# Two-layer hybrid encoder trunk: weights ahead of the second token tile, GpSimd's loads behind ten split chunks, and four splits placed elsewhere in the engines' orders

## What is computed

```python
for i in range(2):
    x = LN(alpha*x + 0.5 * swiglu(x, ffn_w_in[i,0], ffn_w_out[i,0]))        # 1024 -> 2816 -> 1024
    x = LN(alpha*x + token_mix(x, w_in[i], ..., w_br[i], w_out[i]))         # four gated mixers
    x = LN(alpha*x + 0.5 * swiglu(x, ffn_w_in[i,1], ffn_w_out[i,1]))
    x = LN(alpha*x + sigmoid(x @ ple_gate_w[i] + b) * (p[i] @ ple_w[i]))    # embedding
```

## Time and profile before

| what | us |
|---|---|
| three runs | 1456.32, 1460.9, 1455.49; median 1456.32 |
| the profiled execution | 1455.92 |
| its span, first to last instruction | 1454.1 |
| TensorE busy (matmul) | 1420.6 (98%) |
| VectorE busy | 975.9 (67%) |
| ScalarE busy | 664.2 (46%) |
| mean granted TensorE clock | 0.994 |

### The profile page before, as it was taken

How to read it: one execution, slowest core, us unless ns; L and a number is a source line. 1 busy time by engine, 2 the same in 40 slices (tenths; PEclk the granted TensorE clock), 3 DMA queues, 4 the chain that set the end, 5 groups by cost and what they waited for, 6 DMA issues and landing times.

```text
span 1454.1 us, 23318 instructions
## 1 busy us (share of the span) xinstructions
PE 1420.6 (98%) x10174; PEld 1324.2 (91%) x10174; DVE 975.9 (67%) x1085; ACT 664.2 (46%) x653; POOL 53.6 (4%) x100
## 2 busy tenths in 40 slices
PE   8999999999999999999989999999999999999996
PEld 6999989999998889999779999899999998999985
DVE  4544577899786865445874545768997858545477
ACT  4444335664545444443444344347535354443441
POOL 5000000000000010000000000000000001000000
PEclk9999999999999999999999999999999999999999
DMA  9756545546544576565465665554456455755641
GB/s 313 226 183 194 174 150 170 176 151 219 168 129 157 191 245 198 184 193 174 155 221 183 194 189 188 174 175 145 169 179 175 132 174 181 229 184 193 198 150 58
DMA packets 168054, 263.34 MB, mean 181 GB/s; under 512 B 8958, under 2 KB 101456, under 8 KB 167952
## 3 DMA queue, kind: packets, MB, share of 16 engines
q1 hardware_dynamic: 163616, 249.66, 53.3%
q0 software_dynamic: 4336, 12.20, 2.6%
HBM read 260.77 MB, written 1.05 MB: 180 GB/s over the span
## 4 chain that ended last, share of the span: by engine, by line
PE 88%; DVE 7%; DMA 2%; ACT 1%; SPq 0%; issue 0%; DVEq 0%; ACTq 0%
PE ps L1250 27%; PE ps L1252 27%; PE ps L1251 27%; PE ps L1452 3%; DVE wlo L773 3%; DMA raw<-in_ffn_w_in 2%; DVE big L901 2%; PE ps L1276 1%; PE ps L1278 1%; ACT whi L544 1%; PE ps L1281 1%; PE ps L1317 1%; DVE big L837 0%; DVE xlo L814 0%; DVE xtok L842 0%
## 5 line engine op out<-in xcount | busy, mean ns | idle before, releaser
L773 DVE TENSOR_TENSOR wlo<-raw,whi 128x2048 fp32r<-128x2048 f32 x230 | 525.0, 2289 | 334.2 <-ACT whi L544 333.9
L1250 PE MATMUL ps<-xhi,whi 128*128 128x256 f32 x2336 | 658.8, 282 | 3.3 <-DVE S L788 3.3
L544 ACT CAST whi<-raw 128x2048 fp32r<-128x2048 f32 x230 | 438.3, 1909 | 487.1 <-PE ps L1252 455.1
L1252 PE MATMUL ps<-xhi,wlo 128*128 128x256 f32 x2336 | 655.7, 281 | 0.0
L1251 PE MATMUL ps<-xlo,whi 128*128 128x256 f32 x2336 | 655.6, 281 | 0.0
L1250 PEld LDWEIGHTS ps<-xhi,whi 128*128 128x128 f32 x2336 | 441.2, 189 | 6.7 <-DVE wlo L773 2.2
L1251 PEld LDWEIGHTS ps<-xlo,whi 128*128 128x128 f32 x2336 | 441.0, 189 | 1.5
L1252 PEld LDWEIGHTS ps<-xhi,wlo 128*128 128x128 f32 x2336 | 440.9, 189 | 0.0
L1250 PE MATMUL ps<-whi,bh 128*128 128x512 f32 x368 | 146.8, 399 | 2.0 <-DVE blo L804 2.0
L1252 PE MATMUL ps<-whi,blo 128*128 128x512 f32 x368 | 145.2, 395 | 0.0
L1251 PE MATMUL ps<-wlo,bh 128*128 128x512 f32 x368 | 144.7, 393 | 0.0
(11 more groups left out here) (241 smaller groups left out, 1209.0 us busy)
## 6 DMA issues: line engine op xcount, KB each, us to landing
raw<-in_ffn_w_in SPq DMA_DIRECT2D x172, 512.0 KB, 5.0
raw<-in_w_in SPq DMA_DIRECT2D x140, 512.0 KB, 4.5
raw<-in_ffn_w_out SPq DMA_DIRECT2D x88, 512.0 KB, 4.4
raw<-in_w_br SPq DMA_DIRECT2D x32, 512.0 KB, 5.2
raw<-in_w_out SPq DMA_DIRECT2D x16, 512.0 KB, 4.2
raw<-in_ple_gate_w SPq DMA_DIRECT2D x16, 512.0 KB, 4.5
gv<-in_ln_g POOLq DMA_DIRECT2D x8, 512.0 KB, 4.9
b_bc<-in_ln_b POOLq DMA_DIRECT2D x8, 512.0 KB, 6.1
```

The lines of the kernel that those rows point to most:

```text
L544: nc.scalar.copy(whi[:, slot, :], raw[:, source, :]).then_inc(whi_made, 1)
L773: nc.vector.tensor_tensor(wlo[:, slot, :], raw[:, source, :], whi[:, slot, :].bitcast(F32), ALU.subtract).then_inc(wlo_made, 1)
L1250: nc.tensor.matmul(dst, a_hi, b_hi, start=start, stop=False, skip_group_check=True)
L1252: return nc.tensor.matmul(dst, a_lo, b_hi, start=False, stop=stop, skip_group_check=True)
```

## The change

It has five parts. (1) SyncE loads token tile 1 between chunk 0 and chunk 1, not ahead of chunk 0; TensorE turns tile 1 behind the first pass of tile 0, and ScalarE and VectorE split it behind all four half chunks. TensorE runs 14 instead of 8 products of ones behind its first turn. (2) GpSimd waits for ten split chunks ahead of its 37 DMAs. (3) In step 5 of the mixers the subtraction of the mean stands ahead of both `los` calls. (4) At step 0 of a feed-forward half the sixth chunk is split behind the hidden part, on both engines. (5) In norm i=2 the third gate chunk is subtracted ahead of x's tile 1; in the last norm the next layer's chunk 1 is cast ahead of quarter 2's sigmoid and subtracted between quarter 2's gate and its product, and `low_x` of tile 0 stands behind quarter 3's gate.

```diff
@@ SyncE
+                        if c0 + gu_at(j) + kk == 0:
+                            sp.dma_start(xtok[:, 1, :], x[0, P:T, :]).then_inc(x_in[1], 16)
-            for t in range(TT):
-                sp.dma_start(xtok[:, t, :], x[0, P * t:P * t + P, :]).then_inc(x_in[t], 16)
+            sp.dma_start(xtok[:, 0, :], x[0, 0:P, :]).then_inc(x_in[0], 16)
@@ GpSimd
             link(nc.gpsimd.memset(wbd[:, :, :], 0.0))
+            pool.wait_ge(wlo_made, 10)
@@ ScalarE, ffn at j == 0
-                        his(g + RING + 2)
                         if middle is not None:
                             middle()
                         act.wait_ge(h0_T, n0 // NFF + 1)
                         nc.scalar.copy(hhi[0], ...).then_inc(hhi_made, 1)
+                        his(g + RING + 2)
@@ ScalarE, start (VectorE alike, with low_x and head_low)
             split_x(0, 0)
-            head(0)
-            head(1)
+            for i in range(4):
+                head(i)
             split_x(0, 1)
-            head(2)
-            head(3)
@@ ScalarE, last norm
                     if a == 2:
-                        his(base + CHUNKS + 1)
-                    if a == 3:
                         his(base + CHUNKS + 2)
-                        if l + 1 < DEPTH:
-                            split_x(4 * l + 4, 0)
+                    if a == 3 and l + 1 < DEPTH:
+                        split_x(4 * l + 4, 0)
@@ VectorE, ffn
-                    if j == 0:
-                        los(g + RING + 2)
-                        if middle is not None:
-                            middle()
+                    if j == 0 and middle is not None:
+                        middle()
                     dve.wait_ge(hhi_made, n + 1)
                     ...
-                    if j > 0:
-                        los(g + RING + 2)
+                    los(g + RING + 2)
@@ VectorE, norm
-                        los(following + 2 + t)
+                        los(following + 2 + t + (i == 2 and t == 1))
                         low_x(nn + 1, t)
@@ VectorE, mixers
+                    if s == 5:
+                        dve.wait_ge(mean_done, l + 1)
+                        nc.vector.tensor_tensor(yc, yc, ps[:, 6, 0:256]..., ALU.subtract).then_inc(d_made, 1)
                     los(base + gate_chunk(s, 1) + RING)
                     ...
                     los(base + gate_chunk(s, 1) + RING + 1)
                     ...
-                    if s == 5:
-                        (the same two lines)
@@ VectorE, last norm
                     gate(a)
+                    if l + 1 < DEPTH and a == 2:
+                        los(base + CHUNKS + 2)
+                    if l + 1 < DEPTH and a == 3:
+                        low_x(4 * l + 4, 0)
                     ...
                     residual(t, c, e)
-                    if a == 2 and l + 1 < DEPTH:
-                        los(base + CHUNKS + 2)
-                        low_x(4 * l + 4, 0)
@@ TensorE, ffn
-                if n0 > 0:
-                    turn_x(version, 1, xtok)
+                if n0 == 0:
+                    pe.wait_ge(x_in[1], 16)
+                turn_x(version, 1, xtok)
@@ TensorE, start
-            for t in range(TT):
-                pe.wait_ge(x_in[t], 16)
-                turn_x(0, t, xtok)
-            keep_busy(8)
+            pe.wait_ge(x_in[0], 16)
+            turn_x(0, 0, xtok)
+            keep_busy(14)
```

More of the change, by code:

```diff
@@ L957, in _ @@
             low_x(0, 0)
-            head_low(0)
-            head_low(1)
+            for i in range(4):
+                head_low(i)
             low_x(0, 1)
-            head_low(2)
-            head_low(3)
             made[0] = 2
@@ L1116, in _ @@
                         branch_low(0, ps[:, 4:6, :].rearrange("p a (b t) -> p (a b) t", b=2), NB * l + 3)
+                    if s == 5:
+                        dve.wait_ge(mean_done, l + 1)
+                        nc.vector.tensor_tensor(yc, yc, ps[:, 6, 0:256].unsqueeze(1).to_broadcast([P, KW, T]),
+                                                ALU.subtract).then_inc(d_made, 1)
                     los(base + gate_chunk(s, 1) + RING)
@@ L1164, in _ @@
                         conv_taps(l, CONV_OPS)
-                    if s == 5:
-                        dve.wait_ge(mean_done, l + 1)
-                        nc.vector.tensor_tensor(yc, yc, ps[:, 6, 0:256].unsqueeze(1).to_broadcast([P, KW, T]),
-                                                ALU.subtract).then_inc(d_made, 1)
                     if s == 6:
```

## The result

The changed kernel takes 1441.93 us, the median of four runs (1439.97 to 1444.1), against 1456.99 for the kernel before on the same chip (four runs, 1455.49 to 1460.9). The ratio is 0.9887 with a 95% interval of 0.9867 to 0.9907, so it is faster by 1.1%. Its profiled execution took 1442.08 us with a span of 1440.3; that of before 1455.92 and 1454.1. The page's first line answers to the earlier trace rows: TensorE is busy for 1420.0 us where it was for 1420.6, so nearly all of the 13.8 us by which the span is shorter are pauses.

The account below looks back on a forecast made before the run. TensorE, busy 1420.6 of 1454.1 us, was taken as the bound, leaving only pauses and slow clock to win. 5.8 + 1.9 + 1.7 + 1.0 + 0.9 + 3.4 = 14.7 us off 1455.92 gave 1441.2, stated as 1441.5; range 1437.5 to 1449.

Parts of the forecast that it names:

- Part 3: Step 5 of the mixers: TensorE's 2.9 us wait for ScalarE's square goes in both layers, 5.8 us.
- Part 5, gate chunk: Norm i=2: subtracting the third gate chunk in VectorE's idle time removes TensorE's wait in each layer, 1.9 us.
- Part 5, boundary: Boundary of the layers: VectorE's idle time ahead of tile 1 is filled, winning 1.7 us despite a new `low_x` wait.
- Part 4: Second half of layer 1: the hidden part no longer stands behind the late sixth chunk, 1.0 us.
- Parts 1 and 2, the start: Start: chunk 2's cast comes 2.0 us later, but later pauses shrink or go; net win 0.9 us of 6.5.
- Part 2's loads in the steady state: GpSimd's loads, moved to near 55 us, meet the steady weights but are covered: cost 0, upper bound 9.2 us.
- The clock: The two slow stretches behind the pauses of 3.3 and 2.9 us go: 2 x 1.7 = 3.4 us, bounds 0 and 5.1.
- the slow stretches come elsewhere: Rival, whole run: slow stretches stay or come elsewhere, so the win is 11.3 us, giving 1444.6 us; chance 0.25.
- Loads that wait: Rival, near 55 to 85 us: GpSimd's loads make TensorE wait, 4.6 us, giving 1446 us; chance 0.10.
- the seventh product: Rival: the 5.8 us come back as a 2.9 us wait at each layer's seventh branch product, 1449 us; chance 0.07.
- slower by the clock: Rival, whole run: longer unbroken work brings the lower clock more often, 1.7 us per stretch, making it slower; chance 0.03.

Follow-up runs that it names:

- e1_mean: The kernel before with only the mean's subtraction moved ahead of both splits of step 5: 1450.03 us, ratio 0.9952.
- e12_hidden: The kernel before with only the sixth chunk's split moved behind the hidden part: 1453.4 us, ratio 0.9964.
- e5_noorder: The changed kernel with both token tiles again loaded and turned ahead of chunk 0, as before: 1437.33 us, ratio 0.9858.
- e6_product: The changed kernel with each of the first two silu products ahead of the subtraction of a chunk needed later: 1437.28 us, ratio 0.9857.
- e11_tiles: The kernel before with only token tile 1 loaded behind chunk 0 and turned behind the first pass, and 14 products of ones: 1460.44 us, ratio 1.0013.
- e7_rows: The changed kernel without the four 4-row by 256-column products that spread the mLSTM's running maximum: 1438.25 us, ratio 0.9858.
- e10_changed: The changed kernel again, with nothing altered, timed beside later experiments: 1444.36 us, ratio 0.9893.

## Why the prediction was right, point by point

**The total.** 14.7 us were forecast; the profiled pair shows 13.85, the medians 15.06. 1441.93 stands 0.4 from 1441.5. That it is so close is luck: the same kernel timed again had 1444.36, and the start and the clock each hold errors that cancel. The steps named below add up to 14.7; the small shifts of 0.1 us between them take back 0.8. (One sum of the chances is off: half of 0.07 and 0.05 is 0.06, not 0.055.)

**Part 3: right.** Forecast 2 x 2.9, measured 3.05 and 3.03 (3.02 and 3.09 at the instruction itself, in the changed kernel and in e1_mean alike). I had the square end near 440.6 by the clock of before; it ended at 441.86, in an execution that was 1.58 us behind there (the row of 338.21), so within 0.4 of it. TensorE starts 3.2 us later, the foretold cover of 3. The three splits cover themselves, and the seventh branch product moved with TensorE.

**Part 5, gate chunk: right.** 1.9 forecast, both waits gone; TensorE's gain at the two places, 1.37 and 1.17, holds small shifts beside the two waits of 1.0.

**Part 5, boundary: right, a little small.** 1.7 forecast, 2.12 measured, twice. The new wait for `low_x` is 1.3 (1.4 forecast), that for tile 1 1.3 (1.7).

**Part 4: right.** 1.0 forecast in the second half of layer 1, 1.01 measured, 1.02 in e12_hidden.

**Parts 1 and 2, the start: right as a sum, but it hid two opposite terms.** TensorE restarted at 26.54 (27.2 forecast) because chunk 2's cast came at 18.32 (18.9 forecast). The start won 1.11 us in the execution without a slow stretch (0.9 forecast); with the start of before scattering by 2.0 us (39.97, 40.35 and 42.00), that agreement is partly luck. The second silu product was done at 28.9, not 29.8. What I hadn't asked is what each part brings without the other. Part 2 alone wins 4.2 us there; part 1 alone loses 2.1 at the restart; and taken out of the changed kernel its absence wins 2.76 at the restart, which e5_noorder and e6_product show from two sides. I had worked out that chunk 2's cast comes "2.0 us later", and didn't read it as the price of an order that could be had otherwise. The products of ones I had misread as well: each is two records, so six more take 1.3 us and not 0.7, and the 14 ended at 9.5, not before 8. The first half chunk was subtracted by 9.3, so this cost 0.2 us at most.

**Part 2's loads in the steady state: right.** Cost 0 forecast, no wait between 50 and 100 us. The cover I reckoned with, some 12 us over a landing of 5, was used: one chunk took 11.9 us, ScalarE waited 4.22 us for it, and none of that reached TensorE. The Trainium skill (DMA: Bandwidth & Descriptors, section Queues, rings and completion order) has the queues take turns by packet. The trace agrees in that neither queue stood back, and it shows no even turns: from 72 to 80 us GpSimd's queue held 81.7% of the engines and the weights' 14.5%. The rule said nothing of whether that was covered.

**The clock: the step that was mis-sized.** "I take both as gone: 2 x 1.7 = **3.4 us**". Both went, and that at 1011 too: 1.2 + 1.4 + 1.5 = 4.1 us. But one came at 295.9 (1.4 us inside it) and one at the start (1.11 - 0.17 = 0.9 at the product behind it): net 1.8. Each stretch was also held to cost "at least 1.6 us"; the pair shows 1.2 to 1.5, as the products follow each other 1.8 times as slowly in one and not twice. The term treated each stretch as a property of the kernel; the runs show places with a frequency. Over all 14 profiles, worked out from the granted clock:

| place | slow in |
|---|---|
| near 445 and 1164, with the pause for the square | 4 of 10 |
| the same, without it | 0 of 18 |
| near 738, old boundary | 5 of 5 |
| near 738, new boundary | 4 of 9 |
| near 295 and 1005, where no pause stands ahead | 16 of 26 |
| the same, without the 4-row products | 0 of 2 |

The table leaves out the start, where 8 of the 14 profiles have a stretch somewhere between 12 and 32 us, one at 535 us in e11_tiles, and the tail behind the last products.

The first two rows bear out half of the step: with that pause gone the stretch behind it doesn't come. The boundary's is only rarer. Of the rivals, that the slow stretches come elsewhere (1444.6) was partly true in each execution: run again, the changed kernel had a median of 1444.36. Loads that wait, the seventh product, and slower by the clock didn't show.

**Open.** That the 4-row products bring the stretches near 295 and 1005, when they lie whole between two moments at which the clock can change, is what the 26 chances and e7_rows together show; without the products there is only one chance that counts. For the pause of 2.9 us the rows point the same way: in the four chances with a stretch such a moment fell within 0.8 us of an end of the pause or outside it, in the six without one it cut the pause at least 0.9 us from either end. What settles it at the boundary and at the start isn't worked out. Of the 4.3 us by which the five parts alone (20.8) exceed the whole (16.5), the start explains about 2.0 (4.2 - 2.0 + 0.87 of parts 2, 1 and 4, against 1.11), since part 2 alone already takes the hidden part's wait that part 4 takes; the rest lies within the intervals.

**A better kernel.** Two versions beat the kernel before by more than the change does, the changed one without part 1 (1437.33 us) and the changed one with the first silu products ahead of the subtractions (1437.28 us); their ratios are 0.9858 and 0.9857 against 0.9887 and 0.9893 for the changed kernel. The intervals of single kernels touch (0.9878 and 0.988 against 0.9867 and 0.9877 at the ends), but the three kernels in which that pause is shortened all stand between 1437.28 and 1437.92, and the traces show the 2.76 us. Like is compared with like in the profiles that have one slow stretch each: the changed kernel's span is 1438.8 us (e10_changed), those of the two versions are 1435.3 and 1435.2. So the pause, with what hangs on it at the start, is worth about 3.5 us, and the rest of the 4 to 7 us between the medians is not placed. Combining the edits gives no more.

## What to carry to other kernels

A split, a cast or a subtraction that nothing needs yet costs nothing of itself and everything through what stands behind it in its engine's order: find the wait, then ask what stood in front of the late instruction and when TensorE would ask for that. When a change has several parts at one place, price each with the others absent as well, since two parts can hide each other and one of them can be a loss. Where random slow stretches of the clock blur the medians, compare the starts of the same instructions in two traces, count slow stretches as chances over many profiles, not as events of one, and ask where each stands against the moments at which the clock changes. A share or a landing time taken over a long window hides the short stretch in which it is bad.

## What the runs showed that I had not expected

- A slow stretch (granted 0.50, 1.2 instead of 2.4 GHz) came with TensorE busy throughout ahead of it, near 295 and 1005, in 16 of 26 chances. The Trainium skill (TensorE: Matmul & The Clock Gate, Part 1) gives idleness as what brings the reduced clock; the trace agrees at the pauses of 2.7 to 3.3 us and not here, where the rows show no pause. What stands just ahead here is products of 4 rows, and the stretch came each time that the clock's next moment of change lay behind all of them, never when it fell among them.
- A pause of 2.9 us brought one in only 4 of 10 chances, and pauses of 1.3 us at the new boundary in 4 of 9. Behind the old boundary's 3.3 us it came in 5 of 5. A pause raises the chance; where it lies against the moments at which the clock changes seems to decide, as far as the ten chances of the 2.9 us pause go.
- GpSimd's 37 loads held 79.7% of the DMA engines from 22 to 30 us before, and a chunk took some 13.5 us to land. Moved, they were no gentler: 81.7% from 72 to 80 us, and a chunk that took 11.9. Over their whole length they had 30.5% and 31.9%. What changed is that by then the kernel had chunks in hand.
- The kernel before, run again beside the experiments, had medians of 1458.24 to 1459.29 us where its first four runs gave 1456.99: ratios are to be taken against the runs on the same chip alone.
